# Four layers on one core: tiles in SBUF placed at multiples of 32 bytes instead of 128

## The reference

```python
def reference(x, ...):
    h = x + nsa_mixer(rmsnorm(x))          # q,k,v,z = h @ w_in ; 16 heads of 64; @ w_out
    h = h + s5_mixer(rmsnorm(h))           # u,z = h @ w_in ; scan ; gelu ; GLU ; @ w_out
    x = rmsnorm(h, final_norm)
    proj = rmsnorm(x) @ w_in_2             # 1024 -> 9744 columns
    o = stack(retention(...), gla(...), swa_sinks(...))
    merged = sum(sigmoid(gates) * (o @ w_branch))
    x = x + rmsnorm(merged @ w_out_2)
    h = rmsnorm(x)
    return x + rmsnorm((silu(h @ w_gate) * (h @ w_up)) @ w_down)   # 1024 -> 2816 -> 1024
```

## Time and profile before

| | |
|---|---|
| median of 3 runs | 1908.04 us (1907.25 to 1909.96) |
| the profiled execution | 1908.04 us, its span 1906.2 us |
| PE busy | 1802.1 us, 95% of the span |
| DVE, ACT, POOL busy | 970.5, 852.4, 170.3 us |
| granted TensorE clock, mean | 0.983 of full |
| DMA | 181.28 MB, queue 1 busy for 29.1% of 16 engines' span |

### The profile page before, as it was taken

The page is one execution under the profiler, slowest core; times in us unless marked ns, Lnnn a source line. Parts: engine busy times, 40 slices in busy tenths (PEclk is TensorE's granted clock), DMA queues, the critical chain, the costliest instruction groups (busy, mean ns, idle before and its releaser), DMA issues.

```text
span 1906.2 us, 24071 instructions
## 1 busy us (share of the span) xinstructions
PE 1802.1 (95%) x9772; PEld 1449.9 (76%) x9772; DVE 970.5 (51%) x1640; ACT 852.4 (45%) x1437; POOL 170.3 (9%) x293
## 2 busy tenths in 40 slices
PE   6899998899999999999999999999899899999996
PEld 4677786679988877865877778877687678888885
DVE  7878556854854373344345554355534534434223
ACT  6445666645363243334355553365523433323222
POOL 2000226510000000000000000022200001111000
PEclk9899999999999999999999999999999899999998
DMA  4553441044423323211322222211232122332331
GB/s 135 169 197 119 128 111 45 1 137 179 145 96 104 104 88 112 92 44 45 109 86 78 78 78 89 83 65 56 67 100 89 67 78 89 100 99 87 101 100 55
DMA packets 60318, 181.28 MB, mean 95 GB/s; under 512 B 7008, under 2 KB 18080, under 8 KB 57776
## 3 DMA queue, kind: packets, MB, share of 16 engines
q1 hardware_dynamic: 60208, 179.75, 29.1%
HBM read 165.57 MB, written 16.25 MB: 95 GB/s over the span
## 4 chain that ended last, share of the span: by engine, by line
PE 73%; DVE 13%; ACT 9%; POOL 3%; issue 2%; DMA 0%; SPq 0%; DVEq 0%; ACTq 0%
PE bank L901 17%; PE bank L903 17%; PE bank L902 17%; DVE wlo L1951 2%; PE bank L964 2%; PE bank L966 2%; PE bank L965 2%; POOL Ps L2719 2%; PE bank L1127 1%; ACT L1401 1%; PE bank L1106 1%; ACT Ps L1849 1%; ACT whi L1396 1%; PE bank L921 1%; PE bank L922 1%
## 5 line engine op out<-in xcount | busy, mean ns | idle before, releaser
L1951 DVE TENSOR_TENSOR wlo<-wraw,whi 128x1024 fp32r<-128x1024 f32 (+1 forms) x262 | 316.3, 1209 | 324.0 <-ACT whi L1396 322.7
L901 PE MATMUL bank<-Hh,whi 128*128 128x512 f32 (+2 forms) x1104 | 445.6, 404 | 16.3 <-DVE wlo L1951 16.3
L903 PE MATMUL bank<-Hh,wlo 128*128 128x512 f32 (+2 forms) x1104 | 433.8, 393 | 0.0
L902 PE MATMUL bank<-Hl,whi 128*128 128x512 f32 (+2 forms) x1104 | 433.5, 393 | 0.0
L1396 ACT ACTIVATE whi<-wraw 128x1024 fp32r<-128x1024 f32 (+1 forms) x262 | 271.5, 1040 | 293.2 <-PE bank L903 225.6
L901 PEld LDWEIGHTS bank<-Hh,whi 128*128 128x128 f32 (+2 forms) x1104 | 208.2, 189 | 74.7 <-DVE wlo L1951 18.6
L903 PEld LDWEIGHTS bank<-Hh,wlo 128*128 128x128 f32 (+2 forms) x1104 | 207.9, 188 | 46.4
L902 PEld LDWEIGHTS bank<-Hl,whi 128*128 128x128 f32 (+2 forms) x1104 | 208.2, 189 | 45.3 <-issue 2.2
L1401 ACT ACT_TABLE_LOAD x97 | 124.5, 1283 | 2.8 <-DVE epst L1966 1.1
L901 PE MATMUL bank<-Bh,whi 128*128 128x512 f32 x256 | 102.2, 399 | 2.2 <-DVE Bl L2494 2.2
L903 PE MATMUL bank<-Bh,wlo 128*128 128x512 f32 x256 | 100.9, 394 | 0.0
(11 more groups left out here) (370 smaller groups left out, 3037.2 us busy)
## 6 DMA issues: line engine op xcount, KB each, us to landing
wraw<-in_w_o SPq DMA_DIRECT2D x24, 512.0 KB, 3.4
wraw<-in_w_bgate SPq DMA_DIRECT2D x24, 512.0 KB, 3.4
wraw<-in_w_branch SPq DMA_DIRECT2D x24, 512.0 KB, 3.4
wraw<-in_w_fg SPq DMA_DIRECT2D x22, 512.0 KB, 3.4
wraw<-in_w_fu SPq DMA_DIRECT2D x22, 512.0 KB, 3.4
wraw<-in_w_glu SPq DMA_DIRECT2D x16, 512.0 KB, 3.4
wraw<-in_w_fd SPq DMA_DIRECT2D x16, 512.0 KB, 3.5
scratch_CA<-CA SPq DMA_DIRECT2D x4, 1152.0 KB, 6.5
```

The costliest lines, as they stand in the source:

```text
L901: pe.matmul(o, wh[:, cols], hi(k), start=k == 0, stop=False)
L902: pe.matmul(o, wh[:, cols], lo(k), start=False, stop=False)
L903: m = pe.matmul(o, wl[:, cols], hi(k), start=False, stop=k == K - 1)
L1951: dve.tensor_tensor(c.wlo[q][:, 0:n], c.raw[i % RR][:, 0:n], c.whi[q][:, 0:n].bitcast(F32), S_).then_inc(*up(DID, ("wlo", i)))
```

## The change

Two roundings change, in `take` and where the first Region starts. The base of free SBUF is at byte 1121, which both round up to 1152. From there the sizes decide. All tiles up to ident are multiples of 128 bytes and stay where they were. epst takes 32 bytes instead of 128; vecs and everything behind it starts 96 bytes lower. Tiles of 192, 48, 32, 64 or 80 bytes (cs, stp, cd, sink, ss) lower what stands behind them by more: the S5 preparation's par to Cq by 160, pT by 288, Ps, pTs and bs by 160, go and ghr by 192. Tiles inside the space of unmoved ones stay. The number of instructions on each engine, their order, their waits and the transfers are the same.

```diff
@@ -2883,7 +2883,7 @@
 
     def take(self, name, shape, dt=F32):
         t = self.nc.alloc_sbuf_tensor_at(name, shape, dt, offset=self.at)
-        self.at += (int(np.prod(shape[1:])) * 4 + 127) // 128 * 128
+        self.at += (int(np.prod(shape[1:])) * 4 + 31) // 32 * 32
         assert self.at <= 229368, name
         return t
 
@@ -2901,7 +2901,7 @@
 
     def __init__(self, nc, ins, out, plan, ev):
         self.nc, self.ins, self.out, self.plan, self.ev = nc, ins, out, plan, ev
-        r = Region(nc, (nc.sbuf_base + 127) // 128 * 128)
+        r = Region(nc, (nc.sbuf_base + 31) // 32 * 32)
         self.always(r)
         self.first_mixer(r.again())
         self.second_mixer(r.again())
```

## The result

| | before | after |
|---|---|---|
| median of the timed runs | 1909.0 us (4 runs, 1907.25 to 1911.88) | 1923.6 us (4 runs, 1922.24 to 1929.01) |
| the profiled execution, its span | 1908.04, 1906.2 us | 1921.54, 1919.7 us |
| PE busy | 1802.1 us | 1817.0 us |

The change made the kernel slower, by a ratio of 1.0081 (95% interval 1.006 to 1.010); the medians differ by 14.6 us. That rival's mechanism is not the one at work, as the experiments show.

A forecast was written before the change was run, and what follows sets the result against it. The prediction took TensorE to bound the kernel, busy for 1802.1 of 1906.2 us. Its terms for TensorE, DVE with ACT, and transfers summed as 0 + 0 + 0 from 1908.04 us: 1908.0 us predicted, range 1904 to 1914.

The forecast's parts named there:

- The slower rival: On PE, moving operands read in 64-byte pieces, a split one costing 7.1 ns more per matmul: 14.6 us, 1922.6 us; chance 0.04.
- TensorE ... Value taken: 0: Cost of moved starts for 2064 matmuls of 512 columns that stream moved tiles: 0, ends 0 and +1.9 us.
- the nearer row: L1140, every other row starting 64 bytes past a multiple of 128: all 128 matmuls 272 ns at least, 273 median.
- The upper bound: On PE, one more access per matmul at DVE's 0.93 ns, for 2064 matmuls: +1.9 us.
- Its argument against 128-byte pieces: 128-byte pieces would have added 14 ns to half of L1140's matmuls, and there is none.
- The faster rival: Clashes between engines depend on low address bits and the old layout made most of them: 1906.2 us; gain beyond 0.2%, chance 0.04.
- transfers: Loads to moved tiles such as mCA, mT, mW, dist2: value 0, ends 0 and +3.3 us if dist2's landing time doubles.
- the DVE term: DVE and ACT instructions on moved tiles: value 0, as Xs against xt; ends a 1.8 us gain and +0.6 us.
- the mark set for it: Landing of mW above 7.9 us, with a PE wait before L1198 or a later first bs on POOL, would show slower transfers.
- The 16-byte line: SBUF's 16-byte cachelines: a start at a multiple of 32 touches no line more, so the sum is 0.

The follow-up runs named there:

- e3: The kernel before with its first tile 32 bytes later and every tile with it; ratio 0.9998, 1908.17 us.
- e4: The kernel before with tiles streamed as fp32r (except Yh) at multiples of 64 bytes, all others at odd multiples of 32; ratio 1.0098, 1927.75 us.
- e9: The kernel before with 96 bytes left free ahead of whi, so whi, wlo and everything behind them move up; ratio 1.0117, 1928.68 us.
- e13: The kernel before, no tile moved, 19 of 22 weight slices in the feed-forward's last product read 160 bytes earlier; Fh matmul starts 233.7 ns apart.
- e1: The kernel before with both roundings at 64 bytes instead of 128; ratio 1.0078, 1924.57 us.
- e6: The kernel before with F written and read 96 bytes later and B 16 bytes later; matmul starts 233.3 ns (F) and 231.6 ns (B) apart.
- e2: The changed kernel, but epst keeps its 128 bytes, so vecs and all tiles streamed as fp32r stand at their old addresses; ratio 0.9997.

## Why the prediction was wrong

**The step that failed** is "TensorE ... Value taken: 0, as the nearer row shows; ends 0 and +1.9". Measured: 2064 matmuls x 7.6 ns = 15.7 us. Three things were wrong in it.

The row was not near. L1140 and L1205 are plain float32 matmuls with 128 moving columns: two of them start 7 ns apart and such pairs 109 ns apart, 0.85 ns for a column; the ones that fill the kernel are fp32r with 512 columns and take a new column every 0.44 ns. The addresses of these rows even had the differences in question, unnoticed: by the shapes, the moving start less the weights' start modulo 256 takes the values 0, 64, 128 and 192 in L1140 before and 32, 96, 160 and 224 after, and in both traces all pairs but the first of a group have the same 109 ns. L1205 likewise has 269 ns before and after, although mCA0 moved by 96 bytes against Xs0. What such a matmul does not feel says nothing on the fast ones. The trace before held no fp32r matmul of L901 to L903 at another difference than 0: Hh, B, F, Y, qs and the rings all had the same start modulo 256. The step should have called this unmeasured, with a wide end, not bounded by a row of another type.

The upper bound was taken from one more access of DVE, 0.93 ns. Nothing tied that to PE; it was 8 times too small.

The question was put to the wrong quantity. Prediction and rivals asked where an operand starts. What counts is how two operands of the same engine start against each other (e3, e4, e9, e13). Before the change rounding to 128 did not make d a multiple of 256 by itself; the sizes did: from whi at byte 46208 to Bh and Fh at 105600 it is 59392 bytes, 232 x 256.

**The slower rival**, at 0.04, had a price of 7.1 ns and 14.6 us; measured were 7.6 ns and 14.6 us. That is luck: its 64-byte pieces are refuted by e1 (no split piece, 6.6 ns slower) and by e3 (all split, nothing slower). (Its argument against 128-byte pieces took the 0.44 ns a column of the fp32r matmuls to L1140, which has 0.85 for two at once.) Its test in the prediction, "Fh at 396 ns, 0.233 us apart", with Hh still at 389, came true for another reason. A number that fits does not show a mechanism; without e3 the document would tell the wrong one.

**The faster rival** came nearest to the idea, clashes that depend on low address bits. It had the sign wrong. It looked at clashes between engines and took the constant 389 ns of Fh as proof that PE has none; it showed that the old layout had the one value of d, of the 15 measured, without them.

**The rest** held for transfers, and for DVE with the exceptions named above. Xs and CA took their values within 1 ns and xt within 2, but L2235 and L2323 became slower, by 1.1 us together, which the DVE term had not: it looked at the place of DVE's own operands, not at the stream beside them. The moved transfers landed about as before (mT 9.4 against 9.7 us in the median; mW's longest, 8.1 us, is 0.2 above the mark set for it) and no PE wait for them appears; POOL's wait that ends with dist2 is 818.0 us instead of 807.8, because dist2 is issued 9.2 us later (1207.0 against 1197.8); dist and dist2 landed in 4.4 us at most, against 5.4.

**Two reads of one engine.** The Trainium skill (SBUF — State Buffer, § Who interferes with whom) gives PE two read ports, one for the moving operand and one for the weights' load, independent, and says that PE never waits on anyone. This case's runs differ from it: with the same instructions, a difference of 96 bytes between the two reads adds 7.6 ns to 226.7 (the change), and so it does, to 234 ns, where only the weights' side was moved (e9, e13). The 16-byte line (SBUF — State Buffer, § Specifications (TRN2)), by which the sum would be 0 too, is neither confirmed nor refuted by these runs; it says nothing on two streams.

**What stays open.** How the two reads get in each other's way was not shown. That the load of the next weights runs beside the stream is in the timeline, where each weight load starts together with a matmul (1800.16 beside 1800.15 after); that they share something with a period of 256 bytes is an inference from two pairs of values (0 and 256, -96 and +160). Differences between the sampled ones were not tried, and the fp32r matmuls with 512 columns are the only kind at which the effect was seen.

## What to carry to other kernels

When fp32r matmuls with 512 columns follow each other at 0.44 ns a column while the next weights load, place the moving and the stationary tiles so that their starts differ by a multiple of 256 bytes, and check it for slices and for every operand of the sequence; an alignment to 128, or any common alignment, is not enough. A layout change that "only" moves addresses is to be priced by the pairs of operands whose distance it changes, and a row may bound it only if it is of the same data type and rate. A matching total is not yet a cause: one run that moved everything together (e3) refuted the theory that had the right number.

## What the runs showed of the hardware that was not expected

- The effect works with the roles changed. In e9 L964 to L966 stream whi and wlo and load Hh and Hl, so that d is +96 for them; their starts (those with 512 columns) are 230.8, 231.2 and 237.6 ns apart against 227 before, and F at d = +96 in e6 shows 231.2 for L901 and L902 and 237.7 for L903.
- d = 0 is not the best for every shape. The matmuls of L986 with 256 columns are 283 ns long and 120 ns apart before; in e9, at d = +96, L986 to L988 are 119 to 121 apart, so the cost of the 512-column ones is not there, and in e4, at d = +64, L986 has 279 ns and 118:

```profile
L986 PE MATMUL bank<-whi,Hh x128: 276/279/681, 446.0 to 501.3; 128*128 128x256 f32 x128
```

- DVE instructions that take X with a step of 32 bytes change with the place of what PE streams beside them. L2323 (X, unmoved, beside the matmuls that stream Y5r and zyr) has a median of 1148 ns before, in e2 and in e3, 1267 after and 1278 in e1. L2329, which reads X with step 1 in the same stretch, has 752 before and 750 after. X's own address is not it: X stands at the same place in e9, with d = 0, where L2323 has 1148, and in e4, with d = 64, where it has 1222. Whether what counts is PE's d or the distance from DVE's operand to PE's was not separated. After, and in e9:

```profile
L2323 DVE TENSOR_TENSOR X<-X,bank x8: 1104/1267/1307, 680.5 to 718.7; 128x512 f32<-128x512 f32 x8
```
```profile
L2323 DVE TENSOR_TENSOR X<-X,bank x8: 1142/1148/1234, 677.2 to 714.3; 128x512 f32<-128x512 f32 x8
```
